# Weight-sum stores, pool products, first weight loads and the reload of x moved in a single-core decoder-layer kernel

## The reference, cut to what matters

```python
h = rmsnorm(x, g_pre);  z = h @ w_in          # split: q_lat kv_lat k_r z_att u_pool z_pool g_att g_pool
q  = rmsnorm(q_lat) @ w_uq                    # 8 heads; q_abs = q_nope x w_uk, q_r = rope(...)
s  = (q_abs . ckv + q_r . kr) * scale; causal; p = softmax(s); o_lat = p @ ckv      # latent attention
y_att  = ((o_lat @ w_uv) * silu(z_att)) @ w_o_att
p = (causal window means of u_pool, widths 2,4,8,16) - u_pool                     # 4 groups of 128 channels
y_pool = ((p @ w_pool) * pool_scale * silu(z_pool)) @ w_o_pool
x = x + (sigmoid(g_att)*y_att + sigmoid(g_pool)*y_pool) @ w_out;  y = rmsnorm(x, g_final)
```

## Time and profile before

| | us |
|---|---|
| median of 3 runs | 2220.62 (2220.12 to 2221.68) |
| the profiled execution | 2223.91 |
| its span, first to last instruction | 2222.1 |
| PE busy | 2062.3 (93%) |
| DVE busy | 1534.5 (69%) |
| ACT busy | 1153.1 (52%) |
| POOL busy | 425.7 (19%) |

### The profile page before, as it was taken

The page is one execution under the profiler, slowest core; times in us unless marked ns, Lnnn a source line. Parts: engine busy times, 40 slices in busy tenths (PEclk is TensorE's granted clock), DMA queues, the critical chain, the costliest instruction groups (busy, mean ns, idle before and its releaser), DMA issues.

```text
span 2222.1 us, 37796 instructions
## 1 busy us (share of the span) xinstructions
PE 2062.3 (93%) x13465; PEld 1914.7 (86%) x13465; DVE 1534.5 (69%) x3302; ACT 1153.1 (52%) x2324; POOL 425.7 (19%) x511
## 2 busy tenths in 40 slices
PE   7999989878989999987998999899899999999997
PEld 6999878666777888687998998899899999999997
DVE  7777878656768777557757757766676667666664
ACT  5446746444544555554665565566465444444443
POOL 4444244212212110213003102100210101010100
PEclk9999999989999999999999999999999999999999
DMA  8866355233312031455775676677588748474753
GB/s 297 266 207 188 100 145 149 74 103 102 107 53 81 20 114 29 148 153 162 242 231 179 220 238 205 200 232 224 171 277 249 269 132 282 139 259 145 259 166 119
DMA packets 266701, 385.41 MB, mean 173 GB/s; under 512 B 31308, under 2 KB 132564, under 8 KB 265484
## 3 DMA queue, kind: packets, MB, share of 16 engines
q1 hardware_dynamic: 260724, 362.67, 52.9%
q0 software_dynamic: 2304, 12.58, 1.5%
q10 hardware_dynamic: 3488, 7.75, 1.1%
HBM read 296.81 MB, written 86.34 MB: 172 GB/s over the span
## 4 chain that ended last, share of the span: by engine, by line
PE 41%; DVE 6%; issue 3%; ACT 3%; DMA 3%; SPq 1%; POOL 0%; ACTq 0%; DVEq 0%; POOLq 0%
PE b_ps L131 40%; DVE d_wr L93 2%; ACT d_wr L1347 2%; DMA out_y<-d_y 1%; DMA d_olf<-out_olat 1%; PE b_ps L2407 1%; DVE d_pool L93 0%; DVE d_c L2281 0%; DVE d_out L2240 0%; DVE d_ht L93 0%; DVE d_pooled L2294 0%; DMA d_pscale<-in_pool_scale 0%; DVE d_hb L93 0%; DMA d_ws<-out_w_sums 0%; ACT d_p L2063 0%
## 5 line engine op out<-in xcount | busy, mean ns | idle before, releaser
L93 DVE TENSOR_TENSOR d_wr<-d_ws,d_wr 128x512 fp32r<-128x512 f32 x648 | 478.6, 744 | 297.7 <-ACT d_wr L1347 293.4
L1347 ACT ACTIVATE d_wr<-d_ws 128x512 fp32r<-128x512 f32 x648 | 399.8, 628 | 358.7 <-PE b_ps L131 356.5
L131 PE MATMUL b_ps<-d_ht,d_wr 128*128 128x258 f32 x3072 | 402.9, 286 | 13.6 <-DVE d_wr L93 9.4
L131 PEld LDWEIGHTS b_ps<-d_ht,d_wr 128*128 128x128 f32 x3072 | 384.0, 191 | 21.4 <-DVE d_wr L93 16.9
L759 PE MATMUL b_ps<-kt,k_qs 128*128 128x512 f32 (+2 forms) x1520 | 345.7, 377 | 27.1 <-DVE b_top L1142 15.5
L759 PEld LDWEIGHTS b_ps<-kt,k_qs 128*128 128x128 f32 x1520 | 270.9, 193 | 77.5 <-DVE b_top L1142 17.9
L131 PE MATMUL b_ps<-d_hb,d_wr 128*128 128x258 f32 x2304 | 307.2, 288 | 4.2 <-DVE d_wr L93 2.7
L131 PEld LDWEIGHTS b_ps<-d_hb,d_wr 128*128 128x128 f32 x2304 | 293.7, 193 | 6.0 <-DVE d_wr L93 3.9
L93 DVE TENSOR_TENSOR b_pt<-b_ps,b_pt 128x512 fp32r<-128x512 f32 x272 | 182.3, 688 | 142.7 <-ACT b_pt L1100 141.6
L1100 ACT ACTIVATE b_pt<-b_ps 128x512 fp32r<-128x512 f32 x272 | 157.7, 596 | 174.2 <-PE b_ps L1206 122.7
L1206 PE MATMUL b_ps<-b_pt,kv 128*128 128x512 f32 x816 | 231.1, 412 | 0.2 <-DVE b_pt L93 0.2
(11 more groups left out here) (236 smaller groups left out, 2442.5 us busy)
## 6 DMA issues: line engine op xcount, KB each, us to landing
d_ws<-out_w_sums SPq DMA_DIRECT2D x256, 256.0 KB, 3.6
d_ws<-in_w_last SPq DMA_DIRECT2D x200, 256.0 KB, 2.7
d_ws<-in_w_pairs SPq DMA_DIRECT2D x192, 256.0 KB, 2.8
b_quarters<-in_w_pairs SPq DMA_DIRECT2D x16, 1024.0 KB, 7.2
out_w_sums<-b_sums SPq DMA_DIRECT2D x16, 1024.0 KB, 5.0
out_q<-a_qout SPq DMA_DIRECT2D x32, 384.0 KB, 3.9
d_hf<-out_ht SPq DMA_DIRECT2D x32, 258.0 KB, 3.8
out_zs<-d_out SPq DMA_DIRECT2D x32, 258.0 KB, 4.3
```

What stands on the lines that cost most here:

```text
L93: return e.tensor_tensor(low, source, high.bitcast(f32), ALU.subtract)
L131: mm = pe.matmul(out, stationary(a, k), moving(b, k), start=first and k == 0 and a + b == 0, stop=last and k == depth - 1 and a == 1, skip ...
L1347: act.activation(ahead["wr"][s % WR][:, 0, :, :], ahead["ws"][s % WS][:, :, :], ACT.Copy).then_inc(ahead["w_hi"], 1)
```

## The change

In attend the additions come two units sooner on POOL (pair n behind `query_low(n+11)`) and the stores of sums one pass later on SP (pass n+14); the quarters are still loaded in pass n+12, and now wait for the additions of pair n-2 instead of its store. Stores count on semaphores of their own, `sums_out`, which are later used again for two of the four gate buffers. At the end of decode SP also issues the loads of units 6, 7 and 8. The product with `w_pool` moves from slot 5 of block q+3 to slot 1 of block q+4, the scaling into `gpo` from slot 7 of block q+3 to slot 2 of block q+4, and the store of `gpo` from slot (q+4,5) to slot (q+5,1). The reload of x moves from slot 22 to slot 26.

```diff
-FIRST_SUMS = SMALL + 4
+FIRST_SUMS = SMALL + 2
 def load_quarters(n):
-    wait(sp, pair_io[n % 2], 32 * (n // 2))
+    wait(sp, added, 4 * n - 4)
 def store_sums(n):
     sp.wait_ge(added, 4 * n + 4)
-                 ).then_inc(pair_io[n % 2], 16)
+                 ).then_inc(keep["sums_out"][n % 2], 16)
 for u in range(SMALL + 2, units):
     load(u)
     store(u - 6)
-    if FIRST_SUMS <= u < FIRST_SUMS + PAIRS:
-        load_quarters(u - FIRST_SUMS)
-    if FIRST_SUMS < u <= FIRST_SUMS + PAIRS:
-        store_sums(u - FIRST_SUMS - 1)
+    if FIRST_SUMS + 2 <= u < FIRST_SUMS + 2 + PAIRS:
+        load_quarters(u - FIRST_SUMS - 2)
+    if FIRST_SUMS + 4 <= u < FIRST_SUMS + 4 + PAIRS:
+        store_sums(u - FIRST_SUMS - 4)
 def add_quarters(n):
     pool.wait_ge(q_ok, n + FIRST_SUMS + 2)
-    pool.wait_ge(pair_io[n % 2], 32 * (n // 2) + 16)
+    pool.wait_ge(pair_io[n % 2], 16 * (n // 2) + 16)
+    wait(pool, keep["sums_out"][n % 2], 16 * (n // 2))
...
 # decode, SP
             for s in range(WS):
                 load_unit(sp, io, ahead, s)
+            for s in range(LEAD):
+                sp.wait_ge(ahead["w_ok"], s + 1)
+                load_unit(sp, io, ahead, s + WS)
 # merge
-POOLED, POOL_MM = 3, 3
+POOLED, POOL_MM = 3, 4
-        STORE_POOL = {SLOT[g + POOL_MM + 1, 5]: g for g in pool_groups}
+        STORE_POOL = {SLOT[g + POOL_MM + 1, 1]: g for g in pool_groups}
-                if s + WS < UNITS:
+                if LEAD <= s < UNITS - WS:
                     load_unit(sp, io, ahead, s + WS)
-                    if s == tile_slot(c, 11, 0):
+                    if s == tile_slot(c, 13, 0):
                         sp.wait_ge(y_out, 32 * c + 32)
-                if p == 7 and g - POOL_MM in pool_groups:      # DVE, gpo
+                if p == 2 and g - POOL_MM in pool_groups:
-                if p == 5 and g - POOL_MM in pool_groups:      # PE, product with w_pool
+                if p == 1 and g - POOL_MM in pool_groups:
```

More of the change, by code:

```diff
@@ L1027, in _ @@
             for n in range(2):
-                sp.wait_ge(pair_io[n], 16 * PAIRS)
+                sp.wait_ge(keep["sums_out"][n], 8 * PAIRS)
         @block.gpsimd
@@ L1051, in _ @@
             for n in range(2):
-                pool.wait_ge(pair_io[n], 16 * PAIRS)
+                pool.wait_ge(keep["sums_out"][n], 8 * PAIRS)
             for sem_ in stored:
@@ L1847, in merge @@
         gp_in, gp_hi, gp_lo = keep["kr_out"], sem("gp_hi"), sem("gp_lo")
-        gates_in = [sem(f"gates_in{n}") for n in range(4)]
+        gates_in = [*keep["sums_out"], sem("gates_in2"), sem("gates_in3")]
+        GATES_BASE = (8 * PAIRS, 8 * PAIRS, 0, 0)
         ya_ok, yp_ok, m_ok, m_hi, m_lo = sem("ya_ok"), sem("yp_ok"), sem("m_ok"), sem("m_hi"), sem("m_lo")
@@ L2334, in _ @@
                         if kind == "OA" and a == 1:
-                            dve.wait_ge(gates_in[n % 4], 32 * (2 * c + n // 4 + 1))
+                            dve.wait_ge(gates_in[n % 4], GATES_BASE[n % 4] + 32 * (2 * c + n // 4 + 1))
                             dve.tensor_tensor(saf[n % 4][:, :], bank[LAST_BANK[n % 2]][:, 0:T], saf[n % 4][:, :],
@@ L2340, in _ @@
                             gate, other = spf[out_n % 4], saf[out_n % 4]
-                            dve.wait_ge(gates_in[out_n % 4], 32 * (2 * c + out_n // 4 + 1))
+                            dve.wait_ge(gates_in[out_n % 4], GATES_BASE[out_n % 4] + 32 * (2 * c + out_n // 4 + 1))
                             dve.tensor_tensor(gate[:, :], bank[OP_BANK[a]][:, 0:T], gate[:, :], ALU.mult).then_inc(yp_ok, 1)
@@ L2540, in build @@
         keep["qh_in"] = [ctx.enter_context(nc.semaphore(f"k_qh_in{n}")) for n in range(2)]
+        keep["sums_out"] = [ctx.enter_context(nc.semaphore(f"k_sums_out{n}")) for n in range(2)]
         keep["s_ok"] = ctx.enter_context(nc.semaphore("k_s_ok"))
```

## The result

The changed kernel takes 2118.99 us in the median of 4 runs (2114.59 to 2121.43), the kernel before in the same comparison 2221.15 (2220.12 to 2221.98). The ratio is 0.9538, with an interval of 0.9522 to 0.9555. The forecast was 2120, a gain of 101 us against 102 measured. That the sum came out to a microsecond is luck: its largest term was some 20 us too small and its last 16 us too favourable, and these two errors nearly cancelled.

The account below looks back on a forecast made before the run. It took PE, busy 93% of the span, as the bound. Terms of 60 + 40 + 1 + 0 = 101 us off the profiled 2223.91 gave 2122.9, 3.3 above the median, so 2120; range 2098 to 2168.

Parts of the forecast that it names:

- Sums and stores in attention: Attention, 300 to 720 us: SP, held by POOL's additions, issues output stores and query loads late; freeing it gains 60 us.
- eight windows of 4 to 8 us: Attention: behind eight PE waits the granted clock is lower, mean 0.50 to 0.72, losing 13.4 us in all.
- upper bound of 64: Attention: most the sums and stores part could gain, 51 us of PE waits plus 13.4 us of clock.
- What is queued behind the new waits: Attention: POOL's additions wait for quarters SP issues in pass n+12; these are there from the second pair on, cost nothing.
- fourth rival: Attention: POOL stands for quarters issued too late, 12.9 us 16 times, attention gain gone; slower, 2386 us; chance 0.04.
- Pool product: 64 blocks of merge: moved three slots later, the product finds `pooled` ready; gain about 40 us, bounds 15 and 52.
- margin of 4.3 us: Pool blocks: three slots later the low part of `pooled` is ready 4.3 us early, against a longest wait of 3.3.
- Store of the pool result: Merge: `gpo` stored four slots before its next write, before five; nothing counted, bound 1 us in 12 places.
- First weights: Start of merge: three weight loads go out before the small constants ACT waits for; gain 1 us, bounds 0 and 4.
- Reload of x: Five chunks: reload in slot 26, head 5's load landing about as before; value 0, bounds 10.3 us gained, 21 lost.
- third rival: Slot 26: new stalls of 5 to 7 us in three chunks cost up to 21 us; time 2141; chance 0.06.
- sign of being wrong: Five chunks: the prediction would be wrong if PE waited over 5 us a chunk for `d_ols`.

Follow-up runs that it names:

- e1: The kernel before with only the attention part: additions two units sooner, stores of sums one pass later on semaphores of their own; 2145.15 us, ratio 0.9633.
- e7: The kernel before with only the stores of sums one pass later on their own semaphores, additions left where they were; 2152.53 us, ratio 0.9657.
- e8: The kernel before with only the additions two units sooner on POOL, stores of sums left in their pass; 2144.90 us, ratio 0.9628.
- e6: The changed kernel with the loads of weight units 6 to 8 back behind the start of merge; 2120.84 us, ratio 0.9521.
- e9: The changed kernel with the reload of x in slot 27, behind head 5's loads, instead of slot 26; 2105.88 us, ratio 0.9463.
- e12: The changed kernel with y stored in slot 19, x reloaded in slot 24, and the history copy issued in slot 12; 2099.02 us, ratio 0.9420.

## Why the prediction was right, and where it was not

**Sums and stores in attention: right cause, size 60 for 80 to 83.** That SP was held by a wait on POOL, and that the output store and the query loads behind it were late, is shown by e1, and more sharply by e7 and e8, which release SP sooner in two different ways and both find the time. The waits came out as said: 59.3 us of idle went, against 51 that I put down to it plus smaller ones. The clock was mis-sized. I added up eight windows of 4 to 8 us and got 13.4 us; the same matmuls gave back 20.7. I also misread one of the eight: it stands behind no stall, its clock is 1.00 and not 0.72 or less, and it adds nothing, so the 13.4 us come from seven. The two waits of 2.37 and 2.42 us that end at 674.60 and 708.85 had no window; PE ran at 0.57 for 4 us behind each, 3.4 us in all.

```profile
342.00:348.00 6.00, 6.00 (x34) 5.04 (x33) 5.55 (x19) 3.14 (x6) 2.94 (x3) 1.00 0.36 127
...
676.00:680.00 4.00, 4.00 (x18) 3.32 (x17) 2.98 (x7) 0.75 (x2) 0.00 (x0) 0.57 1.04 273
```

Where the other 3.9 us were lost is open. The window of the whole stretch, 300 to 720 us, has a mean clock of 0.92 over 357 us of busy time, up to 29 us at stake; its row was to be had before the change. The upper bound of 64 was then no bound. The 4 us that I took off for a next wait were about what is left: 3.3 us idle. ACT now waits for PE there and not for a store.

**What is queued behind the new waits: right.** POOL stood once for late quarters, 2.8 us, and once until a store of sums had landed, 2.9 us, and PE never waited for it. The fourth rival did not come.

**Pool product: right, 40 for 42.** Of the 42 us 11.8 are busy time, the clock's share, as summed from the windows, and 30.1 are waiting. The margin of 4.3 us against a wait of 3.3 was enough in all 16 blocks. The waits for weights came to 16.0 us instead of the 19 assumed (10.8 + 8), and that is the rest of the difference.

What the pool blocks cost DVE was not removed by the change, only given a longer margin. DVE's timeline of the changed kernel at a window sum (POOL runs one of 1.07 us from 1119.61, and three of 4.57 us together from 1120.76):

```profile
1118.16 0.69 DVE L93 TENSOR_TENSOR d_wr<-d_ws,d_wr 128x512 fp32r<-128x512 f32 x1 [1.10 <-ACT d_wr L1348]
...
1119.72 1.51 DVE L93 TENSOR_TENSOR d_wr<-d_ws,d_wr 128x512 fp32r<-128x512 f32 x1
```

The same operation takes 1.51 us beside the sum and 0.69 alone. The rule of the Trainium skill's page "SBUF — State Buffer", section "SBUF: two separate sides", that a DVE operation with two SBUF inputs and a GpSimd operation reading SBUF exclude each other for a whole instruction, agrees with it.

**Store of the pool result: right.** DVE waited once for the landing, 1.0 us, and PE not at all.

**First weights: wrong, 1 for nothing.** The step that failed is that the small constants would land sooner if three weight loads, which share the DMA engines with them, went out before. With these loads moved, the landing of the pool scale went from 6.10 to 7.06 us; without the move (e6) it is 7.85 against 7.82, and the time is the same.

**Reload of x: wrong, 0 for about 16 us slower.** The step that failed is "the bytes up to that load are the same in both orders, so it should land about as before". The bytes of a chunk are the same. What a load waits for is what is under way at its issue. Before, the reload had the engines from 1859.6, the pooling input and gates followed from 1868.0, and head 5 landed after 5.4 us; after, 1.65 MB of pooling input and gates and 1.69 MB of reload were issued from 1853.6 to 1858.4, in front of head 5. That is 3.3 MB, 10 us at the 334 GB/s that ran from 1853.6 to 1869.6 us. It is the size of the delay and no exact account: counted from 1853.6 these bytes alone would be through at 1863.6, and the load, issued at 1858.85, landed at 1869.6, with a weight unit of 256 KB and its own 206 KB behind them. This was the third rival, with stalls of 5 to 7 us, up to 21 us and a chance of 0.06; the stalls were 2.4 to 5.1 us, and 4.8 us of busy time came on top. The prediction's own sign of being wrong, over 5 us a chunk for `d_ols`, came in two of three chunks (7.4 and 5.6 us). I had the rule in hand and used it only for the rival: the Trainium skill's page "DMA: Bandwidth & Descriptors", section "Queues, rings and completion order", has each engine take a ring's descriptors in order. e9 agrees with it on this kernel: swap the reload and head 5's loads, and 12 us are back.

So the forecast of 2120 took 20 us too little off in attention and left out 16 us that were added in the chunks, and it was right to a microsecond by luck. That the time lay in the range is not luck: the mechanism that carried it, in attention and in the pool blocks, was the one named. A different reload would have put the kernel at 2105, still in the range.

## What to carry to other kernels

When one engine issues all transfers, look at each wait it makes on another engine and ask which store or load stands behind it: 83 us hung here on SP's wait for additions whose store nobody needed soon. When a large transfer is moved, list what is in flight in the ten microseconds before the small load behind it, not what the stage moves in all, and put the load that the bound engine needs ahead of the large one. What stalls cost by the clock is read over the whole stretch, from its mean clock and busy time, and afterwards as busy time for the same count of instructions.

## What the runs showed of the hardware

A 206 KB load landed after 10.8 us when 3.3 MB were ahead of it on its queue, after 4.6 in the median before, and the engines were at 1.01 to 1.03 of their time meanwhile. Behind a reload issued 12 us sooner, the same load landed after 5.4 us. A stall of 5.11 us cost 2.1 us more behind it by the lower clock, and in attention 59 us of stalls cost 20.7 more, a third on top. The pool scale, 128 rows of four numbers, took 6.1 to 8.0 us to land at the start of merge in every kernel here, also without the three early weight loads (e6) and without the copy of the history (e12) beside it.
